# Moving the sample's projections into tile 14's output product in a hybrid decoder step on one core

## The chip, the cores and the metric

The kernel runs on one core of one Trainium2 chip. The metric is device time in microseconds, the median of several runs. A core has five engines with a queue each: TensorE (PE in the profile, its weight loads PEld), VectorE (DVE), ScalarE (ACT), GpSimd (POOL) and SyncE (SP), which here issues nearly all DMAs. Engines wait for each other by semaphores, and each runs its own instructions strictly in the order in which the program lists them.

## The reference

It is one layer of a decoder step, on two inputs: a prompt of 2,048 tokens and a sample of 8 tokens (one for each of 8 sequences), width 1,024.

```
u = rmsnorm(x);  proj = u @ w_in            # one combined projection, 2832 columns
gla: q, k, v, forget gate -> recurrence S_t = diag(a_t) S_{t-1} + k_t v_t^T, o_t = q_t S_t, rmsnorm
swa: 8 query heads on 2 key/value heads, window 128, a learned sink logit per head
h = x + (concat(o_gla * silu(g_gate), o_swa * silu(s_gate)) @ w_out);   y = rmsnorm(h)
```

The prompt starts from a zero state. The sample uses its own GLA state and a cache of 127 older keys and values. Outputs are both y, the new states, and the last keys and values.

## The kernel before

**Tiles.** The prompt is 16 tiles of 128 tokens (`Tile(0)` to `Tile(15)`), written out one after the other. The sample is `S = Tile(16)` with 8 columns. The weights are split once into a high and a low half-precision part and stay in SBUF. A product of two split operands takes three matmuls for each block of 128 inputs: high by high, high by low, low by high (`split_product`, lines 616 to 618).

**Software pipeline.** `body(t)` for t = 0 to 14 does the attention and the GLA part of tile t, the projections of tile t+1 (`sq`, `sklow`, `gv`, `gg`, `sg`), the query/key projection of tile t+2 (`gqk`), the output product of tile t (`out_proj`, halves `y0` and `y1`, each 8 chunks of three 512-column matmuls), and `bc`, which broadcasts the norm factor of tile t+3. After `bc`, DVE scales the input (`scale_u`) and then adds the second half of the output product to the residual (`residual`, L1806), which gives back the bank that the next tile's `scores` write. In `bc`'s place the order was written by hand: it stands after chunk 6 of `y1`. The tail, after the last body, does tile 15 without the transposing DMAs (PE transposes the probabilities and the gated output) and all that is left of the sample: its projections `sklow`, `s_gv`, `s_gates` and `sq`, its attention (`s_scores`, `s_turn_probs`, `s_values`), its outer products (`s_outer`), `s_gla_out`, `s_out_proj` and two sums over partitions.

**Order.** Nothing is scheduled by the hardware across a queue: the lists `body` and the tail, one for each engine, are the order. Two banks of PSUM (`pj`, a ring whose order is the list `pj_filled`) take all projections and nearly all small products of the sample; a unit may be written when the unit two places before it has been read (`wait_free`). Two more (`at_ring`) take scores, GLA level scores and `y0`, `y1`; two more (`tr`) take transposes. The gates of tile t+1 from the GLA decay (`factors`, ten DVE instructions) are made in the body, except for tile 15, whose `factors` stand in the tail between two groups of `row_max`.

**In the tail of DVE** the order is `row_max` 0 and 1, `factors`, `take_pt` 0 and 1, `row_max` 2 and 3, the gate and decay steps, `take_pt` 2 and 3, `assemble_levels`, `final_scale` of tile 14, `gate_window`, the head norm, `scale_rows`, and then the sample's small steps around the end of tile 15. The tile's own end is `residual(t,[1])`, a square sum on ACT, `final_mean`, and `final_scale` (L1819); the sample's is `s_residual` (L1989 on) and `s_final_norm` (last instruction L2011).

Of the kernel before, what the change touches and what calls it, by code (L numbers as in the profile page):

```python
# [24 lines left out]
F16 = mybir.dt.float16  # L25
# [6 lines left out]
P = 128  # L32
# [128 lines left out]
def hymba_step_kernel(nc, xT_d, xq_d, xsT_d, xs_d, w_d, gin_d, gout_d, wgu_d, bg_d, sink_d, normf_d, normfT_d,  # L161
                      state_d, kcT_d, vc_d, sinks_s_d, ident_d, tri_d, lvl_d, leafscan_d, band_d, older_d, window_d,
                      y_d, ys_d, Sp_d, kp_d, vp_d, Ss_d, ksT_d, vs_d):
    with ExitStack() as ctx:
# [13 lines left out]
        u_hi = sb("u_hi", [P, 2, DT, P], F16)  # L178
        u_lo = sb("u_lo", [P, 2, DT, P], F16)
# [117 lines left out]
        for n in range(1, NT - 1):  # L297
# [13 lines left out]
        for n in range(NT):  # L311
# [7 lines left out]
            if on_pe(n):  # L319
# [39 lines left out]
        s_sink_in = sem("sample_sinks_in")  # L359
        s_gv_full = sem("sample_values_summed")  # L360
# [5 lines left out]
                   "ns", "mz", "la", "kT", "mx", "nm", "den", "rden", "pn", "sq", "n0", "n1", "rstd", "on", "gg", "am", "amc", "rsc", "rscs", "og", "hi", "lo",  # L366
                   "isc", "h0", "h1", "hsq", "hsum", "hn0", "hn1", "hr", "hn", "out"]),
               "pool": Events(sem("sample_pool"), ["q2z", "q2a", "q2", "km0", "km1", "sa0", "sa", "qsz", "km2", "km3", "am"])}
# [27 lines left out]
        s_ogh = wpart(DT * NS // 2).bitcast(F16).rearrange("p (d b) -> p d b", d=DT)  # L396
        s_ogl = wpart(DT * NS // 2).bitcast(F16).rearrange("p (d b) -> p d b", d=DT)
# [213 lines left out]
        def _(pe):  # L611
# [331 lines left out]

            def s_gates(f0, f1):

                bank = s_begin("gates") if f0 == 0 else pj.bank("gates", S)
                mm = features(S, bank, f0 * NS, COL["gg"] + f0 * P, f1 - f0, step=NS)
                if f1 == DT:
                    mm.then_inc(pj.full, 1)

# [29 lines left out]
            def s_out_proj():  # L980
                bank = s_begin("y")
                after(pe, "dve_lo")
                for k in range(DT):
                    c = k * P
                    mm = split_product(bank[:, k * NS:k * NS + NS],
                                       [(wo_hi[:, f, c:c + P], wo_lo[:, f, c:c + P], s_ogh[:, f, :], s_ogl[:, f, :])
                                        for f in range(DT)])
                mm.then_inc(pj.full, 1)
# [1386 lines left out]
```

## Time and profile before

| | |
|---|---|
| median of 3 runs | 879.21 us (877.46 to 879.51) |
| profiled execution, its own time | 880.4 us |
| its span, first to last instruction | 878.6 us |
| PE busy | 849.8 us, 97% of the span |
| DVE busy | 676.9 us, 77% |
| ACT busy | 389.6 us, 44% |
| POOL busy | 77.5 us, 9% |

Times in the trace are counted from the start of the span. PE's busy time includes its pipeline: two matmuls that follow each other overlap in it, so a matmul's cost is the distance to the start of the next one. The granted clock is given as a share of full speed: 1.00 is 2.4 GHz and 0.50 is 1.2 GHz.

### The profile page before, as it was taken

The numbers are of one execution on the slowest core, as the hardware profiler recorded it, in microseconds if no ns is written. First come the engines' busy times: TensorE is split into PE (matmuls) and PEld (weight loads), VectorE is DVE, ScalarE is ACT, GpSimd is POOL, SyncE is SP. The second block draws the span as 40 slices with busy tenths as digits, with TensorE's granted clock in tenths as the row PEclk, the third lists the DMA queues.
The fourth block names the chain that finished last, engine by engine and source line by source line (L and its number), as shares of the span: only waits on it lengthen the run. The fifth ranks groups of instructions, "written<-read, shape, count | busy, mean of one in ns | idle before, by whom it ended". The sixth has DMA issues, their size and how long they took to land.

```text
span 878.6 us, 22036 instructions
## 1 busy us (share of the span) xinstructions
PE 849.8 (97%) x8842; PEld 591.4 (67%) x8842; DVE 676.9 (77%) x2211; ACT 389.6 (44%) x1008; POOL 77.5 (9%) x117
## 2 busy tenths in 40 slices
PE   7898999999999999999999999999999999998997
PEld 5885667576766576675767666776757676764765
DVE  5899787968778787869687787878696877774854
ACT  4556454545344444345454444444453544443411
POOL 0041010101000010101010000101010100101300
PEclk7899999999999999999999999999999999998977
DMA  9922001414032131314141321313141402203033
GB/s 373 387 113 74 25 26 25 121 25 121 15 84 62 41 94 49 98 26 120 26 117 18 85 62 37 97 49 96 27 121 26 120 14 38 63 14 120 7 100 129
DMA packets 75747, 71.22 MB, mean 81 GB/s; under 512 B 63807, under 2 KB 65271, under 8 KB 74622
## 3 DMA queue, kind: packets, MB, share of 16 engines
q1 hardware_dynamic: 75358, 69.75, 27.2%
q8 instruction: 70, 1.15, 0.5%
q14 instruction: 31, 0.25, 0.1%
q10 hardware_dynamic: 288, 0.07, 0.0%
HBM read 44.33 MB, written 10.78 MB: 63 GB/s over the span
## 4 chain that ended last, share of the span: by engine, by line
PE 83%; DVE 9%; issue 5%; DMA 1%; ACT 1%; POOL 0%; SPq 0%; POOLq 0%; DVEq 0%
PE bank L616 23%; PE bank L617 23%; PE bank L618 23%; DVE xT L1528 3%; PE bank L811 3%; PE bank L721 3%; PE bank L670 2%; PE bank L833 2%; PE bank L837 2%; DVE flex L1806 1%; PE bank L848 1%; PE bank L797 1%; DMA w_out_hi<-in_w 1%; DVE w_in_hi_lo L1875 1%; DMA ogT_lo<-x_rows 1%
## 5 line engine op out<-in xcount | busy, mean ns | idle before, releaser
L616 PE MATMUL bank<-u_hi,w_in_hi_lo 128*128 128x128 f16 (+1 forms) x1288 | 210.2, 215 | 2.9 <-DVE w_in_hi_lo L1875 2.6
L618 PE MATMUL bank<-u_hi,w_in_hi_lo 128*128 128x128 f16 (+1 forms) x1288 | 210.0, 215 | 0.0
L617 PE MATMUL bank<-u_lo,w_in_hi_lo 128*128 128x128 f16 (+1 forms) x1288 | 209.9, 215 | 0.0
L616 PE MATMUL bank<-w_in_hi_lo,u_hi 128*128 128x512 f16 (+3 forms) x528 | 174.9, 341 | 3.6 <-issue 3.6
L617 PE MATMUL bank<-w_in_hi_lo,u_hi 128*128 128x512 f16 (+3 forms) x528 | 175.2, 340 | 0.0
L618 PE MATMUL bank<-w_in_hi_lo,u_lo 128*128 128x512 f16 (+3 forms) x528 | 175.1, 340 | 0.0
L616 PEld LDWEIGHTS bank<-u_hi,w_in_hi_lo 128*128 128x128 f16 x1288 | 124.2, 98 | 12.1 <-issue 3.2
L617 PEld LDWEIGHTS bank<-u_lo,w_in_hi_lo 128*128 128x128 f16 x1288 | 124.0, 98 | 3.0
L618 PEld LDWEIGHTS bank<-u_hi,w_in_hi_lo 128*128 128x128 f16 x1288 | 124.0, 98 | 0.0
L616 PE MATMUL bank<-w_out_hi,ogT_hi 128*128 128x512 f16 x256 | 99.7, 390 | 2.1 <-DMA ogT_lo<-x_rows 2.1
L617 PE MATMUL bank<-w_out_lo,ogT_hi 128*128 128x512 f16 x256 | 99.7, 389 | 0.0
L618 PE MATMUL bank<-w_out_hi,ogT_lo 128*128 128x512 f16 x256 | 99.3, 388 | 0.0
L618 PEld LDWEIGHTS bank<-w_in_hi_lo,u_lo 128*128 128x128 f16 (+1 forms) x528 | 51.7, 98 | 46.4
L616 PEld LDWEIGHTS bank<-w_in_hi_lo,u_hi 128*128 128x128 f16 (+1 forms) x528 | 51.7, 98 | 45.0 <-issue 6.9
L617 PEld LDWEIGHTS bank<-w_in_hi_lo,u_hi 128*128 128x128 f16 (+1 forms) x528 | 51.7, 98 | 38.0
L1237 ACT ACTIVATE flex<-flex,win_stat 128x128 f32<-128x128 f32 x128 | 49.9, 390 | 43.0 <-DVE win_stat L1701 43.0
L1296 ACT ACTIVATE ogT_hi<-flex 128x1024 bf16<-128x1024 f32 x16 | 16.9, 1056 | 80.3 <-DVE flex L1806 80.3
L2228 POOL TENSOR_TENSOR flex<-flex,win_stat 128x512 f32<-128x512 f32 x16 | 16.7, 1042 | 374.1 <-DVE win_stat L1737 349.4
L1528 DVE SCALAR_TENSOR_TENSOR xT<-xT,u_gain,bank 128x128 f32<-128x128 f32 (+1 forms) x136 | 35.6, 335 | 17.8 <-PE bank L626 17.8
L1725 DVE TENSOR_TENSOR flex<-flex,older_slot 128x512 f16<-128x512 f16 x56 | 22.5, 423 | 33.3 <-DMA flex<-win_p_rows_hi_lo 33.3
L618 PEld LDWEIGHTS bank<-w_out_hi,ogT_lo 128*128 128x128 f16 x256 | 25.6, 100 | 32.0 <-issue 3.0
L1701 DVE CUSTOM_DVE_ANT_0 flex<-bank,band_bf,neg_sinks 128x128 f32<-128x128 f32 x128 | 47.0, 406 | 0.0
(310 smaller groups left out, 1650.7 us busy)
## 6 DMA issues: line engine op xcount, KB each, us to landing
xT<-in_xT SPq DMA_DIRECT2D x16, 512.0 KB, 3.3
x_rows<-in_xq SPq DMA_DIRECT2D x16, 512.0 KB
flex<-in_w SPq DMA_DIRECT2D x4, 2048.0 KB, 10.0
flex<-in_xq SPq DMA_DIRECT2D x16, 512.0 KB, 4.2
out_y<-flex SPq DMA_DIRECT2D x16, 512.0 KB, 3.7
w_out_lo<-in_w SPq DMA_DIRECT2D x2, 2048.0 KB, 12.0
w_out_hi<-in_w SPq DMA_DIRECT2D x1, 2048.0 KB, 10.6
w_out_hi<-in_w SPq DMA_DIRECT2D x1, 1088.0 KB, 7.4
```

The lines of the kernel that those rows point to most:

```text
L616: nc.tensor.matmul(out, a_hi, b_hi, start=start and i == 0, stop=False)
L617: nc.tensor.matmul(out, a_hi, b_lo, start=False, stop=False)
L618: mm = nc.tensor.matmul(out, a_lo, b_hi, start=False, stop=stop and i == last)
L670: mm = nc.tensor.matmul(out[0:w, 0:w], top[:, d, c:c + w], top[:, d, c:c + w], start=d == 0 and c == 0, stop=d == DT - 1 and (c, w) == blo ...
L721: mm = nc.tensor.matmul(at_ring.bank(name, t)[:, i * 2 * P:(i + 1) * 2 * P], q16[r:r + HD, t.p, lq, 2 * pair + i, :], k16[r:r + HD, t.p, l ...
L811: mm = nc.tensor.matmul(bank[:, c:c + P], EX[:, l0 + l, f, :], QE[:, l0 + l, f].rearrange("p h c -> p (h c)"), start=True, stop=True)
L833: nc.tensor.matmul(accG[:, f * 2 * DV:(f + 1) * 2 * DV], EX[:, S_INTER, f, :], S_bd[:, f].rearrange("p h c -> p (h c)"), start=f == 0, sto ...
L837: mm = nc.tensor.matmul(accG[:, h * DV:h * DV + DV], AT[:, h, :], gv[:, t.p, h * DV:h * DV + DV], start=False, stop=h == HG - 1, skip_grou ...
L1237: e = nc.scalar.activation(PR[:, u % 2, i, :], PR[:, u % 2, i, :], ACT.Exp, scale=-1.0, bias=wst[:, 0, k:k + 1], accum_out=wst[:, 1, k:k + 1])
L1528: u = V.scalar_tensor_tensor(out=xT[:, d, 0:n], in0=xT[:, d, 0:n], scalar=ugain[:, d:d + 1], in1=pj.bank("bc", t)[:, 0:n], op0=ALU.mult, o ...
L1701: m = V.tensor_tensor_reduce(PR[:, u % 2, i, :], bank[:, i, P:2 * P], band[:, first], nsig[:, :], nsink[:, k:k + 1], ALU.add, ALU.min, wst ...
L1725: V.tensor_tensor(PT[:, u % 2, 1].rearrange("p l h c -> p (l h) c"), PT[:, u % 2, 0].rearrange("p l h c -> p (l h) c"), bcast(older16[:, : ...
```

## The change

1. `bc(t+3)` is issued after chunk 5 of `y1` and not after chunk 6, in bodies 1 to 13.
2. In body 14, all projections of the sample come before and among tile 14's output product: `sklow` and half of `s_gv` before it, then a piece of `s_gates` or `s_gv` after each chunk of `y0`, then a quarter of `sq` after every second chunk of `y1`. ACT reads them at the end of its body 14.
3. `s_gates` and `s_out_proj` use `stacked`: the sample's high and low parts stand beside each other as 16 moving columns, so that two matmuls do for a block of 128 instead of three; DVE adds the two halves afterwards (`s_sum_gates`, and in `s_residual` one instruction more).
4. `factors` of tile 15 moves from DVE's tail into body 14.
5. The tail has another order on all engines, and the ring `pj` another list. Among it: `s_turn_keys`, `s_turn_low` and `s_gate_up` right behind the first `scores`; ACT's `s_low` before its `probs`; `s_log_gate` before `probs` 2; `s_scores`, `s_turn_probs`, `s_values` and three of the `s_outer` before the transposes of the output; the last three chunks of tile 15's `y1` between the first pieces of `s_out_proj`; DVE's `residual(t)` in one piece behind `s_split_out`.

```diff
         pj_filled += [(u, NT, who) for u, who in (
-            ("kt", "act"), ("sklow", "act"), ("low", "act"), ("z", "dve"),
-            ("gates", "act"), ("sq", "act"), ("kv0", "dve"), ("kv1", "dve"), ("sc", "act"),
-            ("kv2", "dve"), ("pT", "dve"), ("kv3", "dve"), ("o", "dve"), ("pv", "dve"), ("ss", "dve"),
-            ("y", "dve"), ("hs", "dve"))]
+            ("sklow", "act"), ("gates", "dve"), ("sq", "act"), ("kt", "act"), ("low", "act"), ("z", "dve"),
+            ("sc", "act"), ("pT", "dve"), ("kv0", "dve"), ("kv1", "dve"), ("pv", "dve"), ("kv2", "dve"),
+            ("kv3", "dve"), ("o", "dve"), ("ss", "dve"), ("y", "dve"), ("hs", "dve"))]
...
+            def stacked(out, terms):
+
+                last = len(terms) - 1
+                both = out.rearrange("p (l b) -> p l b", l=2)
+                for i, (a_hi, a_lo, b) in enumerate(terms):
+                    if i < last:
+                        nc.tensor.matmul(both, a_hi, b, start=i == 0, stop=False)
+                    nc.tensor.matmul(out[:, 0:NS], a_lo, b[:, 0], start=False, stop=False)
+                    if i == last:
+                        mm = nc.tensor.matmul(both, a_hi, b, start=False, stop=True)
+                return mm
...
+            def sample_projections(t):
+
+                proj(S, "sklow")
+                s_gv(0, 4)
+                for d in range(DT):
+                    out_proj(t, 0, d, d + 1)
+                    if d % 2 == 0:
+                        s_gates(d, d + 2)
+                    else:
+                        s_gv(4 + d // 2, 5 + d // 2)
+                for d in range(DT):
+                    out_proj(t, 1, d, d + 1)
+                    if d % 2 == 0:
+                        s_sq(d // 2)
...
-                    out_proj(t, 0)
-                    out_proj(t, 1, 0, 6)
                     if t.n + 3 <= NT:
+                        out_proj(t, 0)
+                        out_proj(t, 1, 0, 5)
                         bc(t + 3)
-                    out_proj(t, 1, 6)
+                        out_proj(t, 1, 5)
+                    else:
+                        sample_projections(t)
 
             iterations(pe, body)
             t = Tile(NT - 1)
             scores(t, 0)
             s_turn_keys()
-            proj(S, "sklow")
-            s_gv(0, 2)
+            s_turn_low()
+            s_gate_up()
             turn_probs(t, 0)
             turn_probs(t, 1)
             scores(t, 1)
-            s_turn_low()
...
+            s_scores()
             values(t, 0)
             values(t, 1)
...
+            s_turn_probs()
             values(t, 2)
             values(t, 3)
             turn_keys(t)
-            proj(S, "sq")
-            gla_out(t)
             s_outer(0)
             s_outer(1)
-            s_scores()
+            gla_out(t)
+            s_values()
+            s_outer(2)
             turn_out(t, 0)
             turn_out(t, 1)
-            s_outer(2)
-            out_proj(t, 0, 0, 3)
-            s_turn_probs()
-            out_proj(t, 0, 3, 4)
             s_outer(3)
             state_update(t)
             for k in range(4):
-                out_proj(t, 0, 4 + k, 5 + k)
+                out_proj(t, 0, 2 * k, 2 * k + 2)
                 s_gla_out(2 * k, 2 * k + 2)
-            s_values()
-            out_proj(t, 1, 0, 3)
+            out_proj(t, 1, 0, 2)
             s_sum("ss", "dve_sq", s_on[:, 0, :])
-            out_proj(t, 1, 3)
-            s_out_proj()
+            out_proj(t, 1, 2, 5)
+            for k in range(DT):
+                s_out_proj(k, k + 1)
+                if k < 3:
+                    out_proj(t, 1, 5 + k, 6 + k)
...
             s_take_kt()
+            s_low()
             probs(t, 0)
             probs(t, 1)
-            s_take_kv()
             final_root(t + -1)
             probs_hi(t, 0)
             probs_hi(t, 1)
-            s_low()
+            s_log_gate()
             probs(t, 2)
             probs(t, 3)
...
+            def s_sum_gates():
+                pj.wait_full(dve, "sq", S)
+                pj.wait_full(dve, "gates", S)
+                s_freed(V.tensor_reduce(s_graw, pj.bank("gates", S)[:, 0:2 * DT * NS].rearrange(
+                    "p (d l b) -> p d b l", d=DT, l=2), AX.X, ALU.add))
...
             row_max(t, 0)
             row_max(t, 1)
             final_mean(t + -1)
-            factors(t)
+            s_sum_gates()
+            s_window()
             take_pt(t, 0)
             take_pt(t, 1)
             row_max(t, 2)
             row_max(t, 3)
+            s_take_z()
             sink_steps(t)
-            s_take_z()
             assemble_leaves(t)
+            s_log_decay()
             denominators(t)
-            s_log_decay()
+            s_row_max()
             take_pt(t, 2)
             take_pt(t, 3)
+            s_normalise()
+            s_take_probs()
             assemble_levels(t)
...
             s_squares()
-            s_gate_window()
-            residual(t, [0])
             s_mean_squares()
             s_gate_gla()
             s_split_out()
-            residual(t, [1])
+            residual(t)
             final_mean(t)
             final_scale(t)
             s_residual()
```

## Rows read from the trace of the kernel before

**Rows 1.** The page: TensorE's granted clock in 40 equal slices.

```profile
PEclk7899999999999999999999999999999999998977
```

**Rows 2.** PE's waits in the whole execution: us in total, times, longest.

```profile
PE bank L721 <- DVE flex L1806: 5.8, 13, 1.0
...
PE bank L616 <- DMA ogT_lo<-x_rows: 2.1, 1, 2.1
```

**Rows 3.** Windows: stretch, length, busy of PE, PEld, DVE, ACT, POOL; clock, DMA.

```profile
793.60:795.70 2.10, 0.04 (x2) 0.06 (x2) 2.07 (x6) 1.20 (x4) 1.44 (x3) 0.75 0.42 166
795.70:801.40 5.70, 5.70 (x14) 2.05 (x15) 2.09 (x7) 1.63 (x4) 1.59 (x6) 0.50 0.59 194
...
815.00:834.00 19.00, 18.91 (x407) 14.91 (x405) 16.47 (x50) 8.28 (x26) 5.45 (x4) 1.00 0.01 3
...
839.00:849.70 10.70, 9.90 (x45) 6.01 (x44) 6.46 (x20) 1.71 (x5) 0.00 (x0) 0.52 0.20 67
```

**Rows 4.** Timeline of PE: start, us, line, operands, count.

```profile
708.95 0.27 PE L626 MATMUL bank<-rstd_diag,ones 128*128 128x128 f32 x1
...
811.01 0.17 PE L616 MATMUL bank<-u_hi,w_in_hi_lo 128*128 128x8 f16 x1
...
813.19 0.38 PE L616 MATMUL bank<-w_in_hi_lo,u_hi 128*8 128x512 f16 x1
...
833.30 1.11 PE L833 MATMUL bank<-gla_state,flex 128*128 128x256 f32 x4
...
845.43 0.61 PE L616 MATMUL bank<-w_out_hi,ogT_hi 128*128 128x512 f16 x1
...
852.58 0.95 PE L968 MATMUL bank<-u_hi,x_rows 128*128 128x2 f32 x8
853.39 0.38 PE L616 MATMUL bank<-w_out_hi,ogT_hi 128*128 128x512 f16 x1
...
867.74 0.17 PE L616 MATMUL bank<-w_in_hi_lo,w_out_hi 128*128 128x8 f16 x1 [1.04 <-DVE w_in_hi_lo L1983]
```

**Rows 5.** Timeline of DVE; brackets hold the idle time before and its releaser.

```profile
707.95 0.29 DVE L1521 TENSOR_SCALAR rstd_diag<-ident,x_stat 128x128 f32<-128x128 f32 x1
709.45 2.15 DVE L1528 SCALAR_TENSOR_TENSOR xT<-xT,u_gain,bank 128x128 f32<-128x128 f32 x8 [1.21 <-PE bank L626]
...
810.88 0.15 DVE L1694 COPY win_stat<-neg_sinks 128x1 f32<-128x1 f32 x1 [0.90 <-PE bank L721]
...
813.45 0.62 DVE L1618 TENSOR_TENSOR flex<-gla_q,flex 128x256 f32<-128x256 f32 x1
...
818.59 0.42 DVE L1708 SCALAR_TENSOR_TENSOR flex<-bank,flex 128x256 f16<-128x256 f32 x1
...
820.18 0.15 DVE L1694 COPY win_stat<-neg_sinks 128x1 f32<-128x1 f32 x1
...
828.47 1.68 DVE L1712 TENSOR_TENSOR flex<-flex,older_slot 128x512 f16<-128x512 f16 x1
830.08 0.41 DVE L1647 COPY flex<-bank 64x256 f32<-64x256 f32 x1
...
842.55 0.27 DVE L1912 TENSOR_REDUCE w_in_hi_lo<-bank 64x1 f32<-64x128 f32 x1
...
867.58 0.74 DVE L1806 SCALAR_TENSOR_TENSOR flex<-bank,row_unscale,flex 128x512 f32<-128x512 f32 x1
...
870.78 1.28 DVE L1819 SCALAR_TENSOR_TENSOR flex<-flex,h_stat,norm_f 128x1024 f32<-128x1024 f32 x1
872.92 0.22 DVE L1989 TENSOR_TENSOR w_in_hi_lo<-bank,w_in_hi_lo 128x64 f32<-128x64 f32 x1 [0.85 <-PE bank L618]
```

**Rows 6.** Timeline of ACT in the tail.

```profile
811.22 0.36 ACT L1328 COPY u_hi<-bank 8x256 f32<-8x256 f32 x1
812.26 0.40 ACT L1237 ACTIVATE flex<-flex,win_stat 128x128 f32<-128x128 f32 x1 [0.68 <-DVE win_stat L1701]
...
823.69 0.69 ACT L1319 ACTIVATE u_hi<-u_hi 128x16 f32<-128x16 f32 x3
```

More of the change, by code:

```diff
@@ L942, in s_values, with s_sq @@
                 mm.then_inc(pj.full, 1)
+            def stacked(out, terms):
[8 more added lines that the diff above has]
+                return mm
             def s_gates(f0, f1):
                 bank = s_begin("gates") if f0 == 0 else pj.bank("gates", S)
-                mm = features(S, bank, f0 * NS, COL["gg"] + f0 * P, f1 - f0, step=NS)
+                for f in range(f0, f1):
+                    c = COL["gg"] + f * P
+                    mm = stacked(bank[:, f * 2 * NS:(f + 1) * 2 * NS],
+                                 [(w_hi[:, d, c:c + P], w_lo[:, d, c:c + P], u_both[:, :, S.p, d, 0:NS])
+                                  for d in range(DT)])
                 if f1 == DT:
                     mm.then_inc(pj.full, 1)
+            def s_sq(f):
+                bank = s_begin("sq") if f == 0 else pj.bank("sq", S)
+                mm = features(S, bank, f * P, COL["sq"] + f * P, 1)
+                if f == GRP - 1:
+                    mm.then_inc(pj.full, 1)
+            def sample_projections(t):
[11 more added lines that the diff above has]
+                        s_sq(d // 2)
             def s_gv(d0, d1):
@@ L978, in s_sum, with s_out_proj @@
                                  ).then_inc(pj.full, 1)
[L980 to L983, printed above, removed]
+            def s_out_proj(k0, k1):
+                bank = pj.bank("y", S)
+                if k0 == 0:
+                    s_begin("y")
+                    after(pe, "dve_lo")
+                for k in range(k0, k1):
                     c = k * P
[L985 to L988, printed above, removed]
+                    mm = stacked(bank[:, k * 2 * NS:(k + 1) * 2 * NS],
+                                 [(wo_hi[:, f, c:c + P], wo_lo[:, f, c:c + P], s_og16[:, f]) for f in range(DT)])
+                if k1 == DT:
+                    mm.then_inc(pj.full, 1)
             pe.wait_ge(zeros_set, 1)
@@ L1475, in _ @@
             sink_term(t)
-            s_log_gate()
             s_decay()
@@ L1935, in s_gate_window @@
             def s_gate_window():
-                pj.wait_freed(dve, "gates", S)
+                dve.wait_ge(s_gates_done, 1)
                 pj.wait_full(dve, "pv", S)
@@ L1988, in s_residual @@
                 after(dve, "dve_isc")
-                s_freed(V.tensor_tensor(s_y, pj.bank("y", S)[:, 0:DT * NS].rearrange("p (d b) -> p d b", d=DT),
-                                        bcast(s_am[:, 5, :], 1, DT), ALU.mult))
+                s_freed(V.tensor_reduce(s_y, pj.bank("y", S)[:, 0:2 * DT * NS].rearrange(
+                    "p (d l b) -> p d b l", d=DT, l=2), AX.X, ALU.add))
                 pj.wait_freed(dve, "y", S)
+                s_done(V.tensor_tensor(s_y, s_y, bcast(s_am[:, 5, :], 1, DT), ALU.mult))
+                after(dve, "dve_ysc")
                 half = DT // OUT_GROUPS
@@ L2178, in _ @@
             gate_window(t)
+            s_states(0)
             mean_heads(t)
-            s_window()
-            s_states(0)
+            s_states(1)
             gate_gla(t)
             scale_rows(t)
-            s_states(1)
-            s_row_max()
+            s_gate_window()
             take_out(t, 0)
             take_out(t, 1)
-            s_normalise()
             s_states(2)
-            s_take_probs()
             s_states(3)
```

59 lines of the change are left out of this document (26 added, 33 removed).

## The prediction

> **What bounds the kernel now.** I read the granted clock by slice, PE's waits, the windows of the last 90 us, and then the timelines of PE, DVE and ACT there. The slices [rows 1] show the clock below 9 tenths only in the first two and in three of the last four. PE's waits [rows 2] are few: 5.8 us in 13 waits for L1806, 2.1 us for the transposing DMA of tile 14. So between the first and the last tiles PE's own matmuls are the bound, and what a change can take there is a wait. The tail is another thing. From 815 to 834 PE is busy for 18.91 of 19.0 us, but DVE for 16.47 as well [rows 3]: two engines are nearly full side by side, and it has to be asked which chain would be left if PE had less to do. I cut the end at five points: the last gqk matmul of the sample (about 793.6), scores of tile 15 (810.0), its gla_out (833.30), its out_proj (845.43), s_out_proj (867.74), and the end at 878.6 [rows 3, 4, 5]; the 810.0 is DVE's start of 810.88 less the 0.85 that the scores take.
>
> **The broadcast, one chunk sooner.** Twelve of the 13 waits for L1806 are at tile boundaries, (5.8 - 1.0) / 12 = 0.40 us each [rows 2]; the longest, 1.0, is tile 14's and has no broadcast behind it. The chain is bc at 708.95, eight L1528 from 709.45, L1806, scores [rows 4, 5]. A chunk is three 512-column matmuls of 0.216 us, 0.65 us. The diagonal is written by 707.95 + 0.29 = 708.24 [rows 5], and bc could now issue at 708.30: it just holds. The wait of 0.40 goes and 0.2 is left over. Next late is y1's last chunk, which does not move. **-4.8 us** (bounds: -5.6 if the pipeline's modelled ends hide some wait, -3.5 if bc waits 0.1 for its diagonal each time).
>
> **Tile 14's product, 793.6 to scores.** Before: 16.4 us, made of the 2.1 wait, 16 chunks partly at clock 0.50 (795.7 to 801.4, [rows 3]), and 1.0 for L1806. After: sklow 2.2 (811.01 to 813.19, [rows 4]); s_gv 24 x 0.216 = 5.2; gates 128 matmuls and sq 96. An 8-column matmul costs 0.0268: 192 of them from 867.74 to L1989 at 872.92 less 0.04 [rows 4, 5]. So gates 3.4 (5.1 in three matmuls), sq 2.6. Chunks 16 x 0.648 = 10.4 at full clock, since sklow fills the DMA wait; switches between shapes about 0.7; the wait for L1806, now with nothing moved beneath it, again 1.0. Sum 25.5: scores of tile 15 start **9.1 us later**. If the clock falls after gqk's and sklow's narrow matmuls, as it did by 795.7 after them and a wait, 1.5 to 3 more. The gates need gqk's bank, which ACT reads right after tile 15's decays, while PE is still in s_gv. DVE does factors of tile 15 (813.45 to 818.59, 5.1 us, [rows 5]) while it waits for y0, free of charge.
>
> **Scores to gla_out.** Before 833.3 - 810.0 = 23.3. 14 us of PE work are gone from it and 5.1 of DVE's, but what is left is a chain, and two new links are on it. kt's bank is the gates' bank, so s_turn_keys waits for s_sum_gates, which stands behind both row_max and final_mean on DVE; ACT's queue has s_take_kt and s_low ahead of probs 0, and everything of ACT waits with it. Step by step: scores and two row_max 3.4 (to 813.45, [rows 5]); s_sum_gates 0.3 (nearest the 0.27 of L1912, [rows 5]; 0.2 to 0.5); transposes and their signal 0.6; s_take_kt 0.36 and s_low 0.2 [rows 6]; probs 0 and 1, four exponentials with their sums, 1.8 (0.40 each, and read-outs, from 812.26, [rows 6]); final_root and probs_hi 0.8; take_pt 0 and 1, 1.6 (818.59 to 820.18). That is 9.1 to row_max 2, where it was 10.1 with factors inside: of 5.1 us moved, one is kept. From there: row_max 2 and 3 2.6; s_take_z 0.4; now s_log_gate stands ahead of probs 2, so ACT waits for it, 0.7 [rows 6]; probs 1.8; sink and denominators 0.5; s_row_max 0.5; take_pt 2 and 3 3.6, because L1712, 0.43 when POOL is quiet, took 1.68 beside POOL's scaling of the states [rows 5], and POOL's scaling comes here again since denominators release it. To 20.1; before, this point was 830.08, also 20.1. Then before 3.2 to gla_out. After, s_normalise 0.7 and s_turn_probs 0.5, for which PE waits with values 2 and 3, turn_keys and two s_outer queued behind: 2.9 us at full clock, 5.7 at half. PE has stood idle about 3 us behind scores and again before s_turn_probs; before, waits of 0.9 and 0.8 us with narrow products around them were enough for 0.52 over 839 to 849.7 [rows 3]. So 24.2 to 27.0; I take 26.0: **+2.7** (bounds +0.9 to +3.7).
>
> **gla_out to out_proj.** 845.43 - 833.30 = 12.1 [rows 4]. The same steps in the same order on DVE and ACT; s_values and s_outer 2 lie under them. At clock 0.50 gla_out takes 3.8 for 1.9: 0 to +1.9; nearest is the row of 839 to 849.7: **+1.9**.
>
> **out_proj to s_out_proj.** Before 22.3, half of it s_values, s_outer and a queue of chunks between s_gla_out and the sum ss. After: eight chunks 5.2, four s_gla_out of 0.81 (852.58 to 853.39, [rows 4]) 3.2, two chunks 1.3, then ss to L1983 as before, 4.6. 14.3 at full clock; three chunks at half add 1.9 and I take it, as the four chunks from 845.43 had it: 16.2, **-6.1** (bound -8.0).
>
> **s_out_proj to the end.** Before 10.9: 192 matmuls 5.1, then 872.92 to 878.6, 5.7. After: 128 matmuls take 3.4, saving 1.7. But y1's last three chunks lie among its first three pieces, so y1 is full after 3 x 0.43 + 3 x 0.65 = 3.2, and DVE has residual, final_mean and final_scale ahead of s_residual: from L1806 at 867.58 to the end of L1819 at 872.06, 4.5 [rows 5]. s_residual can start 3.3 + 0.2 + 4.5 = 8.0 behind, though the sample's product is ready at 5.4. With 5.7 + 0.3 for the added reduction (its cost 0.2 to 0.5): 14.0; with three chunks at half clock 15.9, PE having idled 2.3 us for L1983. Middle 14.9: **+4.0** (bounds +3.1 to +5.0).
>
> The 64 matmuls saved in each product are worth 1.7 us by 0.0268 each [rows 4, 5]. By the Trainium skill (TensorE: Matmul & The Clock Gate, LDWEIGHTS), loading 128 weight columns takes about 107 ns, and by that, as an estimate, each stacking would be worth 6.8 us. The trace does not agree: it has a load with every one of the 192 matmuls and they follow each other in 27 ns. By the rule the time would be 10 us less than I forecast; I give it no chance.
>
> **Sum.** -4.8 + 9.1 + 2.7 + 1.9 - 6.1 + 4.0 = +6.8 us on the span of 878.6. The profiled execution took 880.4, 1.2 over the median of 879.2, so I set the difference on the median: about 886. The terms taken near their costly ends (clock) can hardly all come together, so I shave 1: **885.0**.
>
> **Rivals.**
> (a) The same chain, but PE's clock stays at full: -4.8 + 9.1 + 0.9 + 0 - 8.0 + 3.1 = +0.3, 879.5. For it: 810 to 815 had a 1.0 us wait and stayed at 1.00. Against: the holes here are three times as long.
> (b) Faster: moving factors shortens DVE's tail by its whole 5.1 us, because ACT gets through kt and low while row_max still runs or in less time than I count. Place: row_max 2 starts 5.0 us after scores and not 9.1, and all that follows with it; with full clock 879.5 - 4.1 = 875.4, and with POOL's scaling out of take_pt's way (2.0) 873.4. It decides where row_max 2 starts less than 6 us after scores.
> (c) The broadcast gives nothing, because the diagonal comes later by as much: 885 + 4.8 = 890.
> (d) The clock also falls in tile 14's product: 885 + 2 = 887; with the main case.
>
> **Chances.** Main case with (d) 0.56, (a) 0.17, (b) 0.23, (c) 0.04. A difference under 0.3% (2.6 us) can't be told from none here. (a) is mostly within; the main case is slower unless half its clock terms are absent. Faster 0.27, same 0.14, slower 0.59. The range runs from 874.5, leaving out the lower part of (b), to 889; the main case's own is 881.5 to 889.
>
> **What the profile after would show.** PE's waits for L1806 down from 5.8 to about 1. No wait at 793.6 and full clock to scores of tile 15, which start near 819 - 4.8 = 814. PE idle some 3 us for s_sum_gates right behind these scores, and DVE idle 3 to 4 us before take_pt 0: if these are missing, (b) is right. Gla_out near 840, clock 0.5 around it. Then s_out_proj 14 to 16 us behind out_proj, and s_residual released by DVE's own queue (L1819) and not by PE. I am wrong if DVE is found busy without a hole between scores and gate_window, or if s_residual waits for PE.

## The result, and the profile after

The changed kernel takes 893.01 us (median of six runs, 889.29 to 895.02), the kernel before 879.28 (six runs, 877.46 to 879.65). The ratio is 1.0155, 95% interval 1.0134 to 1.0175: 13.7 us slower, where +5.8 and 874.5 to 889.0 had been forecast. The profiled execution took 889.29 us and is the fastest of the six. Its span is 887.5, its mean granted clock 0.971; the other five have 0.958 to 0.971. Two more profiles of the same kernel were taken later (after_b and after_c below, 893.86 and 894.26 us); they are nearer the median.

PE's waits in the first profile after (wait, total, times, longest), against [rows 2]:

```profile
PE bank L935 <- DVE w_in_hi_lo L1961: 4.8, 1, 4.8
PE bank L1016 <- DVE w_in_hi_lo L2042: 4.2, 1, 4.2
...
PE bank L907 <- DVE w_in_hi_lo L1933: 2.9, 1, 2.9
...
PE bank L861 <- DVE flex L1815: 2.5, 1, 2.5
...
PE bank L951 <- DVE w_in_hi_lo L2022: 2.3, 1, 2.3
...
PE bank L722 <- DVE flex L1838: 1.0, 1, 1.0
```

The wait for L1806, now L1838, is down from 5.8 to 1.0 us, and the transposing DMA is gone from the list. Five single waits of the tail are new or longer, 16.7 us together. Two are new: the transpose of the sample's keys waits 2.9 us until its gates have been summed (L1933), and the transpose of its probabilities 4.8 us for `s_normalise` (L1961). Three have grown: `turn_out` waits 2.5 us (L1815; 0.8 before), `s_out_proj` 2.3 us (L2022; 1.0 before), and the sample's last sum over partitions 4.2 us (L2042; 1.4 before). The same profile in windows (length, PE busy, instructions, granted clock, DMA share, GB/s), against [rows 3]:

```profile
789.00:814.00 25.00, 24.91 (x371) 1.00 0.33 89
814.00:819.00 5.00, 1.18 (x14) 0.97 0.73 216
819.00:823.00 4.00, 3.51 (x21) 0.50 0.01 2
...
832.00:836.00 4.00, 0.00 (x0) 0.97 0.00 0
836.00:840.00 4.00, 3.97 (x45) 0.50 0.01 4
...
852.00:856.00 4.00, 4.00 (x30) 0.50 0.00 0
...
864.00:868.00 4.00, 4.00 (x29) 1.00 0.96 382
```

Tile 14's product with the sample's projections in it runs without a gap at full clock. Behind it PE is busy for 1.18 of 5 us, and from 832 to 836 for none. Behind each of these two holes the clock is 0.50, its lower level of 1.2 GHz. And PE's timeline at the cuts (start, us, line, shape, what ended the idle time), against [rows 4]:

```profile
814.89 0.83 PE L722 MATMUL bank<-win_k_hi_lo,win_q_hi_lo 64*128 64x256 f16 x12 [0.99 <-DVE flex L1838]
...
841.78 2.08 PE L834 MATMUL bank<-gla_state,flex 128*128 128x256 f32 x4
...
856.01 0.61 PE L617 MATMUL bank<-w_out_hi,ogT_hi 128*128 128x512 f16 x1
...
873.73 0.17 PE L951 MATMUL bank<-w_in_hi_lo,w_out_hi 128*128 128x16 f16 x1 [2.33 <-DVE w_in_hi_lo L2022]
```

The next table cuts the tail of every kernel that was run at its first scores of tile 15 and at gla_out, both from PE's timeline. Idle is the length less PE's busy time; half is the time at half clock, worked out as 2 x (1 - granted clock) x length of the window. It also counts stretches in which PE has nothing to do, such as the last microseconds, where the lower clock costs nothing. Each row is one execution.

```
            scores at   span   scores to gla_out    gla_out to end
                               length idle half     length idle half
before        810.0    878.6    23.3   0.1  0.0      45.3   7.9 22.6
after         814.9    887.5    26.9   9.0 12.9      45.7  12.8 25.6
after_b       816.6    892.1    26.7   8.6 15.5      48.8  10.7 39.1
after_c       817.3    892.5    26.3   8.6 11.6      48.9  10.7 39.1
e_bc          806.5    875.1    23.3   0.1  0.0      45.3   7.8 22.6
e_stack       809.3    876.3    23.3   0.1  0.0      43.7   9.2 18.4
b_plain       804.9    873.0    23.3   0.1  0.0      44.9   7.2 23.3
b_warm        806.4    872.6    23.3   0.1  0.0      42.9   8.3 13.7
e_fill        810.2    883.8    28.3   3.2 20.4      45.3   8.0 22.7
e_fillwarm    810.1    881.8    27.5   1.5 17.0      44.2   8.2 17.7
e_move        815.2    878.3    18.8   6.4 10.2      44.3   8.7 22.1
m_warm        816.0    880.0    18.2   7.7  0.0      45.8   8.4 25.6
a_free        816.8    886.9    24.9   8.2  9.9      45.2  12.9 24.4
a_end         816.8    888.5    26.7   8.7 15.5      45.0   7.9 31.5
a_both        816.2    882.0    25.5   7.5 14.8      40.4   7.9 23.4
a_gla         815.4    892.6    21.5   8.1  6.9      55.7  14.5 39.0
a_warm        816.3    887.9    24.0   2.9  3.4      47.6  11.5 33.3
```

### The profile page after: what moved, and what is told of

Same layout as the page of the kernel before. It is cut to its first block, busy times and chain, and to the rows that moved or that the text cites. A ratio compares the mean times of both kernels' runs of the same rounds, so it can differ in the third digit from the quotient of the medians.

```text
span 887.5 us, 21782 instructions
## 1 busy us (share of the span) xinstructions
PE 851.2 (96%) x8714; PEld 589.3 (66%) x8714; DVE 678.7 (76%) x2213; ACT 389.4 (44%) x1008; POOL 77.5 (9%) x117
## 4 chain that ended last, share of the span: by engine, by line
PE 86%; issue 6%; DVE 5%; ACT 1%; DMA 1%; POOL 1%; SPq 0%; POOLq 0%; DVEq 0%
PE bank L617 25%; PE bank L619 24%; PE bank L618 24%; PE bank L812 3%; PE bank L722 3%; PE bank L834 2%; PE bank L838 2%; DVE w_in_hi_lo L1907 1%; PE bank L849 1%; PE bank L671 1%; DMA w_out_hi<-in_w 1%; PE bank L798 1%; PE bank L627 1%; DVE xT L1560 0%; PE bank L820 0%
## 5 line engine op out<-in xcount | busy, mean ns | idle before, releaser
L617 PE MATMUL bank<-u_hi_lo,w_in_hi_lo 128*128 128x128 f16 (+1 forms) x1224 | 204.0, 217 | 3.1 <-DVE w_in_hi_lo L1907 2.8
L618 PE MATMUL bank<-u_hi_lo,w_in_hi_lo 128*128 128x128 f16 (+1 forms) x1224 | 203.6, 217 | 0.0
L619 PE MATMUL bank<-u_hi_lo,w_in_hi_lo 128*128 128x128 f16 (+1 forms) x1224 | 203.6, 217 | 0.0
L617 PE MATMUL bank<-w_in_hi_lo,u_hi_lo 128*128 128x512 f16 (+3 forms) x528 | 175.1, 341 | 3.6 <-issue 3.6
L618 PE MATMUL bank<-w_in_hi_lo,u_hi_lo 128*128 128x512 f16 (+3 forms) x528 | 175.4, 341 | 0.0
L619 PE MATMUL bank<-w_in_hi_lo,u_hi_lo 128*128 128x512 f16 (+3 forms) x528 | 175.4, 341 | 0.0
L617 PEld LDWEIGHTS bank<-u_hi_lo,w_in_hi_lo 128*128 128x128 f16 x1224 | 118.9, 98 | 12.6 <-issue 3.2
L618 PEld LDWEIGHTS bank<-u_hi_lo,w_in_hi_lo 128*128 128x128 f16 x1224 | 118.7, 98 | 3.4
L619 PEld LDWEIGHTS bank<-u_hi_lo,w_in_hi_lo 128*128 128x128 f16 x1224 | 118.7, 98 | 0.0
L617 PEld LDWEIGHTS bank<-w_in_hi_lo,u_hi_lo 128*128 128x128 f16 (+1 forms) x528 | 51.6, 98 | 47.1 <-issue 9.3
L619 PEld LDWEIGHTS bank<-w_in_hi_lo,u_hi_lo 128*128 128x128 f16 (+1 forms) x528 | 51.7, 98 | 46.8 <-issue 0.8
L618 PEld LDWEIGHTS bank<-w_in_hi_lo,u_hi_lo 128*128 128x128 f16 (+1 forms) x528 | 51.7, 98 | 38.6 <-issue 0.7
L2267 POOL TENSOR_TENSOR flex<-flex,win_stat 128x512 f32<-128x512 f32 x16 | 16.7, 1042 | 369.1 <-DVE win_stat L1769 345.9
L1303 ACT ACTIVATE ogT_hi<-bank 128x128 bf16<-128x128 f32 x64 | 16.8, 277 | 71.7 <-PE bank L838 71.7
```

Source lines behind the costliest of these rows:

```text
L617: nc.tensor.matmul(out, a_hi, b_hi, start=start and i == 0, stop=False)
L618: nc.tensor.matmul(out, a_hi, b_lo, start=False, stop=False)
L619: mm = nc.tensor.matmul(out, a_lo, b_hi, start=False, stop=stop and i == last)
L1303: sq_ = nc.scalar.activation(junk[0:n, h * DV:h * DV + DV], accG[0:n, h * DV:h * DV + DV], ACT.Square, accum_out=ost[0:n, 0, h:h + 1])
```

## The experiments

The kernel before was run beside each group: 879.0 us in the first (22 runs), 879.5 in the second (7), 879.2 in the third (14), 879.1 in the fourth (13).

**Four parts alone.** e_bc is the kernel before with the broadcast a chunk sooner. e_fill is the kernel before with this:

```diff
+                    if t.n == NT - 2:
+                        proj(S, "sklow")
+                        s_gv(0, 4)
                     out_proj(t, 0)
...
-            proj(S, "sklow")
-            s_gv(0, 2)
...
-            s_gv(2, 4)
```

with `factors` of tile 15 and `s_take_kv` in body 14. e_stack is the kernel before with `stacked` in the sample's output product alone. e_move is the changed kernel with the gates summed in body 14 and with the order of the tail as before the change, less what was moved out of it; so it has the broadcast, the moves and both stackings.

> The kernel before with the broadcast alone issued one chunk sooner. Theory (the wait for L1806 at twelve tile boundaries is the only thing that it removes): the changed kernel's last projection of the sample starts 4.0 us earlier than before, so 4.0 us faster, 875.3. Rival (the broadcast only moves the wait to another place in the same tile, and the 4.0 us come from elsewhere): no change, 879.3.

> The kernel before, but sklow and half of s_gv of the sample stand ahead of tile 14's output product, and factors of tile 15 in DVE's body 14; all else in its old place and order. Theory (moved work is free only where it fills the wait for the DMA; there it keeps the clock up too): scores of tile 15 start where they did, near 810, and the tail has 4.8 us less of PE work and 5.1 us less on DVE: 3 to 5 us faster, about 875. Rival (the tail is a chain through ACT whatever PE and DVE have to do): under 1 us faster.

> The kernel before with the sample's output product alone in stacked columns (128 matmuls for 192, one DVE instruction more). Theory (each matmul costs 0.027 us whatever its columns up to 16): -1.7 + 0.3, so 1.4 us faster, 877.9. Rival (16 moving columns or the strided pair of them cost more per matmul): no faster or slower.

> The changed kernel, with all of the sample's projections and factors still moved into body 14, the sooner broadcast and the stacked columns, but with the tail's instructions in the order of the kernel before (without the moved ones), and the gates' sum taken on DVE already in body 14. Theory (moving costs 8.8 us of later scores and gives back 3 in the tail; the new tail order costs the rest): -4.0 + 8.8 - 2.9 - 1.4, about 0.5 us slower than before, 880. Rival (the move itself costs it all, since the tail has holes in either order): 6 us slower or more, 886 to 893.

- e_bc: 875.05 us (871.92 to 876.89, 5 runs), ratio 0.9954 [0.9927, 0.998]. The broadcast alone gives 4.0.
- e_fill: 886.44 (880.26 to 887.06, 6 runs), ratio 1.0073 [1.005, 1.0096]. 7.4 us slower; the theory and the rival both missed it.
- e_stack: 878.33 (875.46 to 879.93, 10 runs), ratio 0.9995 [0.9984, 1.0006]. No difference that can be told.
- e_move: 881.82 (880.11 to 883.04, 10 runs), ratio 1.0035 [1.0025, 1.0045]. 11.2 us of the 13.7 are not in it. That lies between the theory (880) and the rival (886 or more), nearer to the theory.

e_fill is the instructive one. Its windows, and the first waits behind the scores (PE's timeline):

```profile
810.00:814.00 4.00, 1.64 (x16) 0.95 0.00 0
814.00:819.00 5.00, 3.97 (x52) 0.50 0.01 2
819.00:823.00 4.00, 4.00 (x80) 0.50 0.01 4
...
828.00:832.00 4.00, 4.00 (x58) 0.50 0.00 0
```

```profile
813.44 0.50 PE L736 MATMUL bank<-ident,flex 128*128 128x128 f32 x2 [2.10 <-ACT flex L1237]
814.69 0.66 PE L736 MATMUL bank<-ident,flex 128*128 128x128 f32 x2 [0.75 <-ACT flex L1237]
```

`sklow` and two chunks of `s_gv` lay where PE waits for ACT's exponentials. Without them PE stands for 2.1 us, the clock falls at 813.6 and stays at 0.50 until 834, over a stretch of narrow products in which PE is busy all the time. Before, the same stretch ran at 1.00 [rows 3]. Those 20.4 us at half clock go with a longer stretch, although work has left it: scores to gla_out is 28.3 us, not 23.3. DVE's list shows who leads now; it stands for 6.1 us in one wait for PE:

```profile
826.14 0.76 DVE L1637 TENSOR_TENSOR flex<-bank,leaf_mask 128x256 f32<-128x256 f32 x2 [6.09 <-PE bank L797]
```

**Four edits of the changed kernel's tail.** a_free sums the gates in body 14 (there the sum no longer waits for `sq`, and its result has another place in SBUF):

```diff
                         scale_u(t + 3)
+                    else:
+                        s_sum_gates()
                     residual(t, [1])
...
             final_mean(t + -1)
-            s_sum_gates()
```

a_end puts y1 whole ahead of the sample's product:

```diff
-            out_proj(t, 1, 2, 5)
-            for k in range(DT):
-                s_out_proj(k, k + 1)
-                if k < 3:
-                    out_proj(t, 1, 5 + k, 6 + k)
+            out_proj(t, 1, 2)
+            s_out_proj(0, DT)
```

a_gla puts the last values, `turn_keys` and gla_out ahead of `s_turn_probs`, with `s_normalise` and `s_take_probs` behind tile 15's gates on DVE, spreads the sample's outer products among the chunks of `out_proj`, and moves the first two `s_states` behind `take_out`. Its expectation speaks of DVE's steps as left in their order; the edit as run moves them. a_warm adds idle matmuls that nothing reads, and a wait ahead of the scores that they need:

```diff
             t = Tile(NT - 1)
+            pe.wait_ge(s_gv_taken, 1)
             scores(t, 0)
+            warm(12)
             s_turn_keys()
...
             level_scores(t, "L2", 2)
+            warm(20)
             s_turn_probs()
```

> The changed kernel, with the sample's gates summed inside body 14, between the two halves of the residual, instead of behind the row maxima of tile 15. Theory (VectorE's order behind scores(15) costs time): the transpose of the sample's keys no longer waits 2.9 us for the sum at 818.3, it starts within 1 us of the end of the scores, the first hole of TensorE behind the scores shrinks from 2.9 us to about the 2.1 us that the exponentials leave, and the time falls by 2 to 3 us, to about 890.5. Rival (the hole is only moved, since turn_probs waits for the exponentials anyway): under 1 us, 892 to 893.

> The changed kernel, with the last three chunks of y's second half ahead of the sample's output product, as before the change, instead of spread among its first three chunks. Theory (y's last add and its stores, not the sample's product, set the end, as in the prediction's step of +4.0): y1 is full some 3 us sooner, the end 2 to 3.5 us sooner, about 890. Rival (the chunks sit in a full-clock stretch and the end is set by the sample's sums): within 1 us of the changed kernel, 892 to 894.

> The changed kernel, with tile 15's remaining values, gla_out and turn_out ahead of the transpose of the sample's probabilities, and VectorE's and the sample's steps in the same order. Theory (the new tail order puts TensorE behind the sample's softmax at 836.0, a hole of 4.8 us, and the clock falls at 835.9): gla_out starts some 5 to 7 us sooner, the hole goes, and the time falls by 4 to 7 us, to about 887.5. Rival (the softmax's wait only moves behind gla_out and the clock falls there instead): 0 to 2 us, 891 to 893.

> The changed kernel with 12 idle matmuls of 512 columns (2.6 us at 0.213 us each) behind the first scores of tile 15 and 20 (4.3 us) ahead of the transpose of the sample's probabilities, in the two holes of 2.9 and 4.8 us; nothing reads them. Theory (TensorE's clock, half for 31 us of the tail, is a large part of the cost): the granted clock stays at 1.00 from 814 to about 849, the PE stretches 819 to 826 and 836 to 846 take some 3 and 5 us less, of which VectorE's waits give half back, 4 to 6 us in all, about 888. Rival (waits for VectorE and ScalarE set this stretch, the clock is only their mirror): under 1.5 us, 891.5 to 893.5.

- a_free: 887.35 (886.74 to 888.76, 4 runs), ratio 1.009 [1.0075, 1.0105]; 5.7 under the changed kernel's median, more than expected. The transpose of the keys now starts 0.76 behind the scores (816.83, 817.59), and the first wait for the exponentials is 0.92. Its profile against after_b's shows where the time went: scores to gla_out is 24.9 us and not 26.7, and out_proj to s_out_proj 15.9 (855.94 to 871.84) and not 19.8, since the clock is back at 1.00 by 859.2.
- a_end: 890.03 (886.42 to 893.38, 4 runs), ratio 1.0116 [1.0079, 1.0153]; 3.0 less, as the theory had it, though its interval and the changed kernel's still overlap. One profile shows where they lie. Up to s_out_proj it is after_b over again (26.7 to gla_out, 19.8 from out_proj to s_out_proj); behind it, 10.9 us are left (877.59 to 888.5), as in the kernel before, and not 14.8.

```profile
877.59 0.17 PE L951 MATMUL bank<-w_in_hi_lo,w_out_hi 128*128 128x16 f16 x1 [0.40 <-DVE w_in_hi_lo L2019]
```

- a_gla: 894.34 (893.72 to 895.63, 4 runs), ratio 1.0169 [1.0154, 1.0184]; not faster. gla_out comes 5.4 us sooner behind the scores (21.5 for 26.9), but the stretch behind it grows by 10.0, to 55.7. It came out nearer the rival: a wait for `s_normalise` now stands behind gla_out (2.1 us), and of the 55.7 us 39 are at half clock. My theory, that the tail loses because the sample's softmax lies ahead of gla_out, isn't borne out, but it isn't refuted either: the edit also made DVE take the softmax later (841.83, and 832.84 in the first profile), so two causes are mixed.
- a_warm: 886.23 (885.76 to 890.9, 4 runs), ratio 1.0087 [1.006, 1.0114]; 6.8 less, for 32 matmuls of extra work. The profiled run is the slowest of the four (890.9, mean clock 0.968; the other three took 885.8 to 886.3 at 0.976). In it the clock stayed at 1.00 only to 823.9, and was at 0.50 to 827.3 and again from 844.4 to 864.9; scores to gla_out went from 26.9 to 24.0. The idle matmuls only add work and move nothing else forward, and still the time falls. So the clock is a cause and not only a mirror of the waits.

**Sum, and the other side.** a_both is a_free and a_end together. e_fillwarm is e_fill with idle matmuls ahead of its hole:

```diff
                 tr.wait_free(pe, name, t)
-                act_w.wait(pe, f"p{u}", t)
                 bank = tr.bank(name, t)
+                if t.n == NT - 1 and u == 0:
+                    warm(bank, 8)
+                act_w.wait(pe, f"p{u}", t)
```

b_plain is the kernel before with the broadcast sooner and the stacked output product, nothing moved. b_warm is b_plain with four idle matmuls in `s_scores` and four in the first `turn_out`, each ahead of the wait.

> The changed kernel with the edits of a_free (the gates summed in body 14) and of a_end (y whole ahead of the sample's output product) together. They gave 5.7 and 3.0 us apart. Theory (two costs of their own, which add up): 884 to 885, and what is left to e_move's 881.8 is the front part of the tail order. Rival (both gains are the same half-clock time, recovered once): 887.

> The kernel of e_fill (before, with the sample's low-rank and first value projections ahead of tile 14's output product, 886.4 us) with 8 idle matmuls of 512 columns (1.7 us) in the 2.1 us hole ahead of the first transpose of the probabilities; nothing reads them. Theory (that hole, with only narrow work behind it, is what drops the clock at 813.8 for 20 us): the clock stays at 1.00 from 810 to about 835 and gla_out comes some 4 to 5 us sooner, about 881. Rival (the long half-clock stretch comes from the missing fillers further on, not from the hole): the clock falls all the same, within 1 us of 886.4.

> The kernel before with the broadcast one chunk sooner and the sample's output product with stacked columns, none of the moves. Theory (the two add up: 4.0 and 0.9 us as measured alone): 874.5. Rival (less narrow work at the end changes nothing there): 875.5.

> b_plain with 4 idle matmuls of 512 columns (0.85 us at full clock) ahead of the wait of the sample's scores and 4 ahead of the wait of turn_out, in the two holes of 0.9 and 0.8 us before which the clock falls at 839 in the kernel before. Theory (the 10 us at half clock from 839 to 849 cost up to 5 us): the clock stays up there and the time falls by 2 to 4 us against b_plain, about 871.5. Rival (the clock falls all the same, because of the narrow matmuls of 8 rows ahead of the hole, and the dummies at half clock outlast the holes): 0 to 2 us slower than b_plain.

- a_both: 883.86 (883.19 to 884.69, 4 runs), ratio 1.0055 [1.004, 1.007]. 9.1 under the changed kernel; 5.7 + 3.0 = 8.7, so the two add up. Its four runs all lie below a_free's four, so a_end's edit counts here too, by 3.5 us.
- e_fillwarm: 882.83 (876.82 to 885.4, 10 runs), ratio 1.0034 [1.0008, 1.0059]; 3.6 under e_fill. Its ten runs lie apart by their clock: 876.82, 877.6 and 878.1 us with a mean clock of 0.979 to 0.981, and 883.7 to 885.4 with 0.968 to 0.971 (five runs). The profiled one, 883.7, is of the second kind: its clock still fell, at 816.7. The three quickest are no gain over the kernel before: its own executions at a mean clock of 0.981, three of the 56 run beside these kernels, took 874.9 to 875.2. So the fill costs some 2 us where the clock holds, and 4.5 to 6 against the median of before where it does not.
- b_plain: 873.31 (870.49 to 875.39, 4 runs), ratio 0.9932 [0.9906, 0.9959]. The lowest median of this study, 5.9 us under the kernel before; its runs overlap with e_bc's (871.92 to 876.89).
- b_warm: 875.85 (874.4 to 877.21, 5 runs), ratio 0.9964 [0.995, 0.9978]. The median is 2.5 us over b_plain's, although in the profiles its tail is shorter (gla_out to end 42.9 and 13.7 us at half clock, for 44.9 and 23.3), and the times overlap. What the idle matmuls are worth here stays open.

**The changed kernel again, and the moves with the hole filled.** after_b and after_c are the changed kernel itself, one profiled run each. m_warm is e_move with the same eight idle matmuls as e_fillwarm.

> The changed kernel itself, profiled again. Theory (the median's other 3.7 us are TensorE's clock, half for longer in the tail): if this execution is one of about 893 us, its half-clock time behind 814 us is some 10 us more than the 31 of the first profile, as one stretch that goes on past 863, with the same waits of TensorE. Rival: new waits, on a DMA or on VectorE, of 3 us or more, at the same half-clock time.

> The changed kernel itself, profiled a third time: as after_b. If both executions are near 889 us, they show only how far one profile repeats (the stage lengths within 0.5 us).

> The kernel of e_move (the moves, the broadcast and the stacked columns with the tail's old order, 881.8 us) with 8 idle matmuls of 512 columns (1.7 us) in the hole of 2.1 us ahead of the first transpose of tile 15's probabilities; nothing reads them. Theory (the moves themselves are near neutral, the clock that falls at 819 for 10 us costs some 3 us, as 8 such matmuls gave 3.6 back to e_fill): about 878.5. Rival (the waits of TensorE at 828 to 836 take what the clock gives): 881 to 882.

after_b took 893.86 us (span 892.1, clock 0.958), after_c 894.26 (892.5, 0.960). Windows of after_b:

```profile
840.00:844.00 4.00, 4.00 (x34) 0.50 0.25 104
...
852.00:856.00 4.00, 3.49 (x24) 0.50 0.00 0
...
860.00:864.00 4.00, 4.00 (x15) 0.50 0.53 180
864.00:868.00 4.00, 4.00 (x15) 0.50 0.72 278
```

In the first profile the clock came back at 846 for 3.4 us and then at 863 for the rest of `out_proj`; here it is at 0.50 in one stretch from 834.7 to 868.8. The waits of PE in the tail are the same or shorter:

```profile
PE bank L935 <- DVE w_in_hi_lo L1961: 4.8, 1, 4.8
PE bank L1016 <- DVE w_in_hi_lo L2042: 4.0, 1, 4.0
...
PE bank L907 <- DVE w_in_hi_lo L1933: 2.9, 1, 2.9
...
PE bank L951 <- DVE w_in_hi_lo L2022: 2.3, 1, 2.3
...
PE bank L861 <- DVE flex L1815: 0.5, 1, 0.5
```

```profile
857.50 0.61 PE L617 MATMUL bank<-w_out_hi,ogT_hi 128*128 128x512 f16 x1
...
877.29 0.17 PE L951 MATMUL bank<-w_in_hi_lo,w_out_hi 128*128 128x16 f16 x1 [2.34 <-DVE w_in_hi_lo L2022]
```

From out_proj to s_out_proj, 17.7 us in the first profile are 19.8 here, 877.29 less 857.50. Scores to the end is 75.5 us and not 72.6. The other 1.7 us lie ahead of the scores (816.6, not 814.9), 1.2 of them in a wait for the weights' DMA at the start (2.8 us for 1.6); the mean clock of the first 100 us is 0.90 there, for 0.93. The theory stands for the larger part: the median's extra time is mostly clock. after_c has the long stretch too (838.8 to 869.6), and one more, in tile 14's product, right behind narrow matmuls with no gap between them (length, PE busy, instructions, granted clock, DMA share, GB/s):

```profile
787.91:791.00 3.09, 3.09 (x122) 1.00 1.05 249
791.00:794.40 3.40, 3.40 (x29) 0.50 0.17 58
```

m_warm: 881.69 (879.24 to 883.17, 10 runs), ratio 1.0037 [1.0018, 1.0056], the same as e_move. The eight matmuls do keep the clock up: no half-clock time to gla_out, for 10.2 us. But the stage is only 0.6 us shorter (18.2 for 18.8), since PE stands idle there for 7.7 us: 4.8 of them wait for DVE and ACT, and for 2.8 ahead of gla_out the profile names no releaser. The rival was right: with the projections gone, this stretch is no longer PE's.

## Why the prediction was wrong

What was measured by medians adds up in this order, each kernel against the one before it: broadcast and stacked output product -6.0 (before to b_plain), the moves, with the gates stacked, +8.5 (to e_move), the tail's order but for two of its parts +2.0 (to a_both), and these two, the gates' sum late on DVE and y's last chunks among the sample's product, +9.2 (to the changed kernel). That is +13.7.

By the prediction's steps, with the first profile and then after_b:

- *Broadcast, -4.8.* Right in mechanism, 0.8 too large. e_bc gave 4.0 in the median, and in the first profile the sample's gqk projection starts 3.95 us sooner (787.12 for 791.07; 788.80 in after_b, 787.91 in after_c). The wait is gone from every boundary, and 1.0 is left at tile 14, as written. Rival (c) is out.
- *Tile 14's product, +9.1.* Right: 814.89 - 787.12 = 27.8 for 19.0 before, +8.8; 24.91 of 25 us busy at clock 1.00. after_b has 27.8 as well (788.80 to 816.58). But after_c has 29.4, +10.5: there the clock is at 0.50 from 791.0 to 794.4. That is rival (d), with 1.6 us for the 1.5 to 3 written, in one of three executions (a_free's profile, 29.4, has it too).
- *Scores to gla_out, +2.7.* Right in mechanism, a little small: +3.6, +3.4 and, in after_c, +3.0. `s_turn_keys` waited 2.9 us for `s_sum_gates`, row_max 2 started 8.85 us behind the scores (9.1 written), and rival (b) is out. `s_turn_probs` waited 4.8 for `s_normalise`. That the total comes so close is in part luck. The steps that I listed from row_max 2 to the end of take_pt 3 add up to 19.2 us behind the scores and not to the 20.1 written, and that point came at 17.95 (832.84 less 814.89). The softmax's three steps then took 3.0 us (832.84 to 835.88) for 0.7: I had not priced that POOL's scaling of the states would hold up DVE's tiny steps too (below). And all that PE had queued behind them ran at half clock, 5.75 us (836.03 to 841.78), my dear bound of 5.7, where the 26.0 took a middle.
- *gla_out to out_proj, +1.9.* +2.1 in both (856.01 - 841.78 and 857.50 - 843.27 are 14.2).
- *out_proj to s_out_proj, -6.1.* **This is the term that failed.** -4.6 in the first profile, -2.5 in after_b. I let the clock come back after three chunks of 512 columns, "as the four chunks from 845.43 had it". In the first profile four chunks and one and a half `s_gla_out` ran at half clock, until 863; in after_b six chunks and two and a half, until 868.8, and such a `s_gla_out` takes 1.6 us for 0.8. The 14.3 us at full clock were right: 17.7 less half of the 7.0 us at half clock is 14.2, and 19.8 less half of 11.3 is 14.1. What was mis-sized is the 1.9 for the clock, which cost 3.5 and 5.6 us. In a_free and a_both, where the gates are summed early, the clock was back sooner (859.2, 857.8) and the stretch took 15.9 and 15.2 us; in a_end it took 19.8. Why the clock came back sooner there isn't shown. The row of before showed one recovery and said nothing of how it repeats, and I took its length for a constant.
- *s_out_proj to the end, +4.0.* +2.9 in the first profile, +3.9 in after_b (892.1 less 877.29 is 14.8; I had written 14.9, the middle between full clock and three chunks at half). a_end confirms the cause: with y1 whole before `s_out_proj` this stretch takes 10.9 us. The mechanism is as written: `s_residual` is released by DVE's own queue, behind `final_scale`, with no idle time ahead of it:

```profile
877.07 0.75 DVE L1838 SCALAR_TENSOR_TENSOR flex<-bank,row_unscale,flex 128x512 f32<-128x512 f32 x1 [2.76 <-PE bank L619]
...
880.28 1.28 DVE L1851 SCALAR_TENSOR_TENSOR flex<-flex,h_stat,norm_f 128x1024 f32<-128x1024 f32 x1
881.48 0.28 DVE L2028 TENSOR_REDUCE w_in_hi_lo<-bank 128x64 f32<-128x128 f32 x1
```

- *The sum.* The terms gave +6.8 and the first profile +8.9. I then set the difference on the median and shaved 1 because the clock terms "can hardly all come together". They came together, and more: after_b is 13.5 above the span of before. Of the 7.9 us between the +5.8 forecast and the +13.7 measured, some 3.6 are the failed term (-2.5 for -6.1), 0.8 the broadcast, 0.8 scores to gla_out, 1.0 the shaving, and up to 1.7 the start of the kernel, which differs from one execution to the next. The range's upper end, 889, is near the sum of every term's dear bound but for this one (-3.5 + 9.1 + 3.7 + 1.9 - 6.1 + 5.0 = +10.1, 889.3): I had given that term a bound only on its cheap side (-8.0).

So the sign came out of the right chain, and the size failed on the clock. The stacked columns changed nothing that can be told: e_stack is within its interval of no change, and in its profile the stretch from gla_out is 1.6 us shorter, with 4.2 us less at half clock, which is what one execution differs by. The Trainium skill (TensorE: Matmul & The Clock Gate, LDWEIGHTS) would have given each stacking 6.8 us as an estimate; the runs do not agree: the whole of e_stack's difference is 0.7 us.

Why the moves cost 8.5: they put some 14 us of matmuls (the prediction's count) into a stretch where PE is the bound, and take them out of one where PE's projections filled the waits of a chain through DVE and ACT. PE's idle time between scores and gla_out is 0.1 us before, 6.4 in e_move, 9.0 in the changed kernel. Against the kernel before, the first stretch grew by 8.8 us, less than the 14 since the matmuls also fill the 2.1 us wait for the DMA and keep the clock up there, and the second lost only 4.5 of its length. From b_plain's profile to e_move's it is +10.1 (17.66 and 27.78), -4.5, and -0.6 behind gla_out: 5.3 us of span. The other 3 us of the 8.5 are no stage of their own: e_move's profile is the fastest of its ten runs, 1.7 under their median, and b_plain's is 1.5 above its own.

What stays open: which part of the tail's order makes up the 2.0 us, what makes the clock come back sooner or later in one and the same kernel, and why b_warm's shorter tail does not show in its median.

## What to carry to other kernels

Work that an engine does while a chain through other engines runs is free where it lies; moved into a stretch where that engine is the bound it costs its length less the waits that it fills there (here 8.8 us for some 14), and the old place gives back only what the chain leaves, here 4.5. A hole of 2 us or more with narrow matmuls behind it had a second price in these kernels, the clock of the next 7 to 34 us: give each clock term of a forecast a bound on its dear side too, and do not shave the sum. Compare executions at a like mean clock before you call one kernel faster. And when an edit bundles moves, an order and a small separate gain, time the small gain alone: the broadcast, one number in two calls, gave 4.0 us by itself, and with the output product stacked the kernel is 5.9 us faster than before.

## What the runs showed of the hardware

**DVE's smallest operations can pay for POOL too.** DVE and POOL in the first profile after:

```profile
831.24 1.68 DVE L1744 TENSOR_TENSOR flex<-flex,older_slot 128x512 f16<-128x512 f16 x1
832.84 1.86 DVE L1957 TENSOR_TENSOR w_in_hi_lo<-w_in_hi_lo 64x1 f32<-64x1 f32 x1
834.73 0.15 DVE L1959 RECIPROCAL w_in_hi_lo<-w_in_hi_lo 64x1 f32<-64x1 f32 x1
834.92 0.96 DVE L1961 TENSOR_SCALAR w_in_hi_lo<-w_in_hi_lo 64x128 f32<-64x128 f32 x1
```

```profile
830.67 1.97 POOL L2321 TENSOR_TENSOR x_rows<-x_rows,u_hi_lo 128x1024 f32<-128x1024 f32 x1
832.60 2.09 POOL L2321 TENSOR_TENSOR xT<-xT,u_hi_lo 128x1024 f32<-128x1024 f32 x1
```

An addition of 64 x 1 takes 1.86 us beside POOL's 128 x 1024 multiplication, and so it does in the profiles of after_b, after_c, a_free, a_end, a_both and a_warm. In a_gla, where the same step comes after POOL's, it takes 0.14:

```profile
841.83 0.14 DVE L1959 TENSOR_TENSOR w_in_hi_lo<-w_in_hi_lo 64x1 f32<-64x1 f32 x1
...
842.20 0.28 DVE L1963 TENSOR_SCALAR w_in_hi_lo<-w_in_hi_lo 64x128 f32<-64x128 f32 x1
```

So a small operation can pay as much as a wide one; 1.7 us of the 4.8 us wait for the softmax are this one addition. Not each of them pays: L1953, a `TENSOR_SCALAR` of 64 x 1 with its start inside POOL's operation of 829.54 to 830.58, took 0.20 us, as in the kernel before, where POOL was quiet.

**The same kernel, the same waits, another clock.** The changed kernel's tail had 37.8 us at half clock in one execution and 54.4 and 49.6 in two others (scores to end; 12.9 + 25.6, 15.5 + 39.1 and 11.6 + 39.1 by the two parts of the table, whose clocks are rounded). Of e_fillwarm's ten executions three took 876.8 to 878.1 us at a mean clock of 0.980 and five 883.7 to 885.4 at 0.969. A clock of 0.011 less over 880 us is 2 x 0.011 x 880 = 19 us more at half, and the means of the groups are 7.4 us apart, so each of them cost about 0.4 us here, as an estimate. The kernel before gives the same way: of its 56 executions run beside the others, the four at 0.980 to 0.981 took 875.2 us on average and the five at 0.973 took 879.8, 4.6 us for 14 us at half, 0.3 for each.
